# A mixture-of-experts stage whose down product goes from fp32 to three fp32r products, with the splits that this needs

## The reference

```python
for each expert e, on the rows routed to it:
    gu   = xs @ w_gu[e] + b_gu[e]                  # 1024 -> 2048
    gate = min(gu[:, :1024], 7);  up = clip(gu[:, 1024:], -7, 7)
    act  = gate * sigmoid(1.702 * gate) * (up + 1)
    out  = act @ w_down[e] + b_down[e]             # 1024 -> 1024
    y[token] += prob * out
```

## Time and profile before

| | us |
|---|---|
| median of 3 runs | 2609.05 |
| lowest and highest | 2608.40, 2609.14 |
| the profiled execution | 2608.08 |
| its span in the profile | 2606.5 |
| PE busy | 2402.0 (92%) |
| DVE busy | 1387.5 (53%) |
| ACT busy | 1117.0 (43%) |
| POOL busy | 587.7 (23%) |
| mean DMA rate | 232 GB/s, 604.43 MB |

### The profile page before, as it was taken

The page is one execution under the profiler, slowest core; times in us unless marked ns, Lnnn a source line. Parts: engine busy times, 40 slices in busy tenths (PEclk is TensorE's granted clock), DMA queues, the critical chain, the costliest instruction groups (busy, mean ns, idle before and its releaser), DMA issues. The chain is left out here.

```text
span 2606.5 us, 36290 instructions
## 1 busy us (share of the span) xinstructions
PE 2402.0 (92%) x11130; PEld 1541.8 (59%) x11131; DVE 1387.5 (53%) x1994; ACT 1117.0 (43%) x1443; POOL 587.7 (23%) x843
## 2 busy tenths in 40 slices
PE   8599999999976599999999999999999999999975
PEld 1177677777843356556556576666565665666641
DVE  0134445444334555555567566656575565666646
ACT  0023333333221445445455455555454554555532
POOL 0132333333221212112112122121221212121110
PEclk9799999999577799999999999999999999999985
DMA  8840000000021878777788789988787797989845
GB/s 307 334 161 33 33 32 32 32 28 3 29 68 38 318 293 296 262 275 282 261 333 331 296 322 348 359 306 309 281 335 284 249 370 263 353 330 366 341 162 220
DMA packets 142976, 604.43 MB, mean 232 GB/s; under 512 B 20128, under 2 KB 25261, under 8 KB 104469
## 3 DMA queue, kind: packets, MB, share of 16 engines
q1 hardware_dynamic: 120311, 551.51, 54.2%
q0 software_dynamic: 21968, 50.99, 8.1%
q10 hardware_dynamic: 662, 1.50, 0.2%
HBM read 561.82 MB, written 42.30 MB: 232 GB/s over the span
## 5 line engine op out<-in xcount | busy, mean ns | idle before, releaser
L1709 DVE TENSOR_TENSOR lo<-raw,hi 128x1024 fp32r<-128x1024 f32 x600 | 716.7, 1222 | 227.7 <-ACT hi L1645 201.5
L1645 ACT ACTIVATE hi<-raw 128x1024 fp32r<-128x1024 f32 x600 | 612.8, 1054 | 200.9 <-PE pg L1595 197.5
L1529 PE MATMUL py<-raw,aT 128*128 128x512 f32 x1184 | 537.9, 599 | 6.3 <-ACT aT L1657 6.3
L1592 PE MATMUL pg<-hi,xs 128*128 128x512 f32 x1184 | 475.4, 401 | 0.0
L1593 PE MATMUL pg<-lo,xs 128*128 128x512 f32 x1184 | 463.5, 391 | 0.0
L1595 PE MATMUL pg<-hi,xs 128*128 128x512 f32 x1184 | 368.1, 392 | 0.0
L1529 PEld LDWEIGHTS py<-raw,aT 128*128 128x128 f32 x1184 | 214.1, 190 | 250.6 <-issue 238.3
L1592 PEld LDWEIGHTS pg<-hi,xs 128*128 128x128 f32 x1184 | 222.5, 188 | 91.7 <-issue 46.7
L1595 PEld LDWEIGHTS pg<-hi,xs 128*128 128x128 f32 x1184 | 222.6, 188 | 50.0
L1593 PEld LDWEIGHTS pg<-lo,xs 128*128 128x128 f32 x1184 | 222.7, 188 | 45.0
L392 PE MATMUL X<-hT,w_in 128*128 128x128 f32 (+1 forms) x1728 | 225.4, 290 | 0.8 <-issue 0.8
(11 more groups left out here) (293 smaller groups left out, 2590.0 us busy)
## 6 DMA issues: line engine op xcount, KB each, us to landing
raw<-in_w_gu SPq DMA_DIRECT2D x300, 1024.0 KB, 7.3
raw<-in_w_down SPq DMA_DIRECT2D x148, 1024.0 KB, 6.9
wada<-in_w_ada SPq DMA_DIRECT2D x12, 2048.0 KB, 7.7
w_in<-in_w_in SPq DMA_DIRECT2D x5, 2048.0 KB, 14.2
moe_rows<-zero SPq DMA_DIRECT2D x9, 512.0 KB
x<-in_x_prompt SPq DMA_DIRECT2D x8, 512.0 KB
w_out<-in_w_out SPq DMA_DIRECT2D x1, 4096.0 KB, 24.8
xr<-in_x_prompt SPq DMA_DIRECT2D x8, 512.0 KB, 3.8
```

Source lines behind the costliest of these rows:

```text
L1529: return pe.matmul(py[n][:, :], aT[:, kt, :], raw[KT + kt // 2][:, kt % 2, n * 512:(n + 1) * 512], start=(kt == 0), stop=(kt == KT - 1))
L1592: pe.matmul(pg[u][b][:, :], xs[:, kt, 0, :], wh[:, u, :], start=False, stop=False)
L1645: act.activation(hi[q % RING][:, :, :], grain(q), ACT.Copy).then_inc(s["hi"], 1)
L1709: dve.tensor_tensor(lo[q % RING][:, :, :], grain(q), hi[q % RING][:, :, :].bitcast(F32), ALU.subtract).then_inc(s["lo"], 1)
```

## The change

All of it is in `experts`:

- An item has 24 grains now (`GRAINS = 3 * KT`): 16 of gate/up (`GU`), and eight of down, grain 16 + kt being row kt of raw8 to raw11. They go through the same rings, and `wait_used` asks for PE's use of a grain; for the last, grain 23, that is `y_mm1`, the end of the item's last product.
- `down` becomes `down_hi` (two products a half) and `down_lo` (one): 48 fp32r products an item in place of 16 fp32 ones.
- `aT` has a hi and a lo part; DVE makes the lo part with a new `act_lo`, once for each half.
- ACT splits grains 8 to 18 before the first swiglu (8 to 15 before), 19 and 20 after it, 21 to 23 later, and then grains 0 to 7 of the next item. DVE follows in the same order, and makes `sel` of the next item (`select`) ahead of the next item's grains, not behind them.
- In a T item PE does `tail_down` in two groups of 16 products, at kt 0 and 4, in place of four groups of 8.
- ACT copies both halves of the output. `y` is now `act1` itself, and the tail result goes to `pair`, a buffer that gate and up share; a wait for the scatter of the item before is added ahead of the tail's swiglu.
- Each item of ACT begins with a sigmoid of one value, `spark`.

```diff
-    GRAINS, RING = 2 * KT, 8
+    GU, GRAINS, RING = 2 * KT, 3 * KT, 8
...
+        sig, pair = sb("sigm", [P, 512]), sb("pair", [P, FF])
+        gate, up = pair[:, 0:512], pair[:, 512:1024]
-        aT = sb("aT", [P, FT, P])
-        y = sb("y", [P, D])
+        aT = sb("aT", [P, FT, 2, P], F32R)
+        y = act1
...
+        def chunk(q):
+            return ORDER[q][0] if q < GU else KT + (q - GU) // 2
...
+        def wait_used(eng, i, q):
+            if q < GRAINS - 1:
+                eng.wait_ge(s["used"], i * (GRAINS - 1) + q + 1)
+            else:
+                eng.wait_ge(s["y_mm1"], i + 1)
...
-            def down(i, kt, n):
-                return pe.matmul(py[n][:, :], aT[:, kt, :], raw[KT + kt // 2][:, kt % 2, n * 512:(n + 1) * 512],
-                                 start=(kt == 0), stop=(kt == KT - 1))
+            def down_hi(kt, n):
+                q = GU + kt
+                pe.matmul(py[n][:, :], aT[:, kt, 0, :], hi[q % RING][:, n, :], start=(kt == 0), stop=False)
+                pe.matmul(py[n][:, :], aT[:, kt, 0, :], lo[q % RING][:, n, :], start=False, stop=False)
+            def down_lo(kt, n):
+                return pe.matmul(py[n][:, :], aT[:, kt, 1, :], hi[(GU + kt) % RING][:, n, :], start=False, stop=(kt == KT - 1))
...
+                    pe.wait_ge(s["lo"], i * GRAINS + GU + kt + 1)
                     for n in range(2):
-                        last = down(i, kt, n)
-                    if kt % 2:
-                        last.then_inc(s["dn_done"], 1)
+                        down_hi(kt, n)
+                    if kt % 4 == 0:
+                        pe.wait_ge(s["alo"], i * 2 + kt // 4 + 1)
+                    for n in range(2):
+                        last = down_lo(kt, n)
+                    last.then_inc(s["used"], 1)
+                pe.wait_ge(s["lo"], i * GRAINS + GRAINS)
                 for n in range(2):
                     for kt in (KT - 2, KT - 1):
-                        last = down(i, kt, n)
+                        down_hi(kt, n)
+                        last = down_lo(kt, n)
+                        if n and kt == KT - 2:
+                            last.then_inc(s["used"], 1)
                     last.then_inc(s[f"y_mm{n}"], 1)
...
             def split_hi(i, q):
                 if q >= RING:
-                    act.wait_ge(s["gu_done"], i * GRAINS + q - RING + 1)
+                    wait_used(act, i, q - RING)
...
             def item(i, tail):
+                act.activation(spark[:, 1:2], spark[:, 0:1], ACT.Sigmoid)
...
-                for q in range(4, RING):
+                split_hi(i, GU + 7)
+                for q in range(RING):
                     split_hi(i, GRAINS + q)
                 if tail:
                     act.wait_ge(s["yt_mm"], i + 1)
                     for n in range(4):
-                        last = act.activation(act1[0:TAIL, n * W:(n + 1) * W], pg[1][0][n * TAIL:(n + 1) * TAIL, 0:W], ACT.Copy)
+                        last = act.activation(pair[0:TAIL, n * W:(n + 1) * W], pg[1][0][n * TAIL:(n + 1) * TAIL, 0:W], ACT.Copy)
                     last.then_inc(s["y_t"], 1)
                 act.wait_ge(s["y_mm0"], i + 1)
                 act.wait_ge(s["y_out"], i * 32 + 32)
                 act.activation(y[:, 0:512], py[0][:, :], ACT.Copy).then_inc(s["y0"], 1)
+                act.wait_ge(s["y_mm1"], i + 1)
+                act.activation(y[:, 512:1024], py[1][:, :], ACT.Copy).then_inc(s["y1"], 1)
...
+            def act_lo(i, b):
+                dve.wait_ge(s["aT"], i * 2 + b + 1)
+                dve.tensor_tensor(aT[:, b * 4:b * 4 + 4, 1, :], pt[0][:, :].rearrange("p (k t) -> p k t", k=4),
+                                  aT[:, b * 4:b * 4 + 4, 0, :].bitcast(F32), ALU.subtract).then_inc(s["alo"], 1)
```

More of the change, by code:

```diff
@@ L1613, in item @@
                         pe.wait_ge(s["aT"], i * 2 + 2)
-                    if tail and kt % 2 == 0:
+                    if tail and kt % 4 == 0:
                         if kt == 0:
                             pe.wait_ge(s["aT_t"], i + 1)
-                        tail_down(kt)
-                        tail_down(kt + 1)
-                    for n in range(2):
-                        last = down(i, kt, n)
-                    if kt % 2:
-                        last.then_inc(s["dn_done"], 1)
[L1623 to L1626, removed]
+                        for c in range(2):
+                            pe.wait_ge(s[f"raw{KT + kt // 2 + c}"], i * 16 + 16)
+                        for k in range(4):
+                            last = tail_down(kt + k)
+                        if kt:
+                            last.then_inc(s["yt_mm"], 1)
+                    pe.wait_ge(s["lo"], i * GRAINS + GU + kt + 1)
+                    for n in range(2):
+                        down_hi(kt, n)
[5 more added lines that the diff above has]
+                pe.wait_ge(s["lo"], i * GRAINS + GRAINS)
                 for n in range(2):
                     for kt in (KT - 2, KT - 1):
-                        last = down(i, kt, n)
+                        down_hi(kt, n)
+                        last = down_lo(kt, n)
+                        if n and kt == KT - 2:
+                            last.then_inc(s["used"], 1)
                     last.then_inc(s[f"y_mm{n}"], 1)
@@ L1640, in split_hi @@
             def split_hi(i, q):
-                kt, b = ORDER[q % GRAINS]
-                act.wait_ge(s[f"raw{kt}"], (i + q // GRAINS) * 16 + 16)
+                act.wait_ge(s[f"raw{chunk(q % GRAINS)}"], (i + q // GRAINS) * 16 + 16)
                 if q >= RING:
-                    act.wait_ge(s["gu_done"], i * GRAINS + q - RING + 1)
-                act.activation(hi[q % RING][:, :, :], grain(q), ACT.Copy).then_inc(s["hi"], 1)
+                    wait_used(act, i, q - RING)
+                act.activation(hi[q % RING][:, :, :], grain(q % GRAINS), ACT.Copy).then_inc(s["hi"], 1)
             def rows_hi(item, half):
@@ L1662, in item @@
                     act.activation(xs_t[:, :, :], pt[0][:, 0:KT * TAIL].rearrange("p (k t) -> p k t", k=KT), ACT.Copy).then_inc(s["xt"], 1)
-                for q in range(RING, GRAINS):
+                for q in range(RING, GU + 3):
                     split_hi(i, q)
@@ L1671, in item @@
                 squash(i, 0)
-                for q in range(3):
-                    split_hi(i, GRAINS + q)
+                for q in range(GU + 3, GU + 5):
+                    split_hi(i, q)
                 act_cols(i, 0)
@@ L1708, in split_lo @@
                 dve.wait_ge(s["hi"], i * GRAINS + q + 1)
[L1709 removed]
+                dve.tensor_tensor(lo[q % RING][:, :, :], grain(q % GRAINS), hi[q % RING][:, :, :].bitcast(F32), ALU.subtract).then_inc(s["lo"], 1)
             def rows_lo(item, half):
```

49 lines of the change are left out of this document (24 added, 25 removed).

## The result

The changed kernel takes **2631.8 us** (median of four runs, 2628.9 to 2632.2) where the kernel before took 2608.7 (2608.4 to 2609.1) on the same chip: ratio 1.0084, 95% interval 1.0069 to 1.0099, so it is slower by 0.8%. The forecast was 2589, the range ended at 2616. The profiled execution took 2631.49 us, its span 2629.9.

A forecast was written before the change was run, and what follows sets the result against it. TensorE (PE) was taken to set the pace in every item. Terms -103.6 + 22.5 + 38.2 + 20.4 + 2.4 = -20.1 us took the profiled 2608.08 to 2588.0; with the runs' median 1.0 higher, 2589 us, range 2561 to 2616.

The forecast's parts named there:

- Part 1: Down products on PE as 48 fp32r in place of 16 fp32: gain 2.80 us an item, 103.6 us in all.
- part 3: New PE wait for DVE's actm in N items: 0.9 us each, loss 22.5 us, N item 37.8 us.
- Part 2: Eight more splits an item on DVE and ACT: costed at nothing, DVE busy 36.4 us, ACT about 29.5.
- Part 4: PE waits at the end of T items for ACT's late tail copies: 3.55 or 2.45 us each, loss 38.2 us.
- Part 5: Clock drop after each of 12 gaps, at half of 3.4 us each: loss 20.4 us, bounds 0 and 41.
- the clock falls for twice as long: Rival: clock drops last twice as long, or also follow the 0.9 us waits: 2609 us, no change; chance 0.13.
- Part 6: The rest: output copies by ACT lose 2.4 us once; sigmoid nothing; selection free where it stands, a loss if moved.
- Part 7: Transfers: an N item's 13.8 MB need 36.3 us, under 37.8, so they cost nothing, by 1.5 us.
- slower, by transfers: Rival: weights arrive no faster than 348 GB/s, N items stay at 39.7 us: 2636 us; chance 0.07.

The follow-up runs named there:

- run 8: The changed kernel with ACT's tail copies ahead of the last four splits and the spark tile allocated last: 2535.8 us, ratio 0.9715.
- run 1: The changed kernel with ACT's four tail copies ahead of the last four of eight splits, not behind all eight: 2552.9 us, ratio 0.9786.
- run 5: The changed kernel with the 8-byte spark tile allocated behind all other tiles: 2612.0 us, ratio 1.0008.
- run 11: The changed kernel with DVE's selection put back behind the lo splits of the next item's first eight grains: 2855.6 us, ratio 1.0936.
- run 9: The kernel of run 8 with PE's transposes of the second actm half behind three down rows, not two: 2520.4 us, ratio 0.9661.
- run 2: The changed kernel with 24 useless transposes on PE at the end of each T item, tail copies still late: 2588.7 us, ratio 0.9919.
- run 12: The kernel of run 9 with the two branch bodies written in the other order, T body first: 2518.9 us, ratio 0.9658.
- run 10: The kernel of run 8 without the sigmoid on spark that begins each item's ACT work: 2535.1 us, ratio 0.9714.
- run 6: The kernel before with an unused 8-byte tile allocated ahead of idx: 2622.3 us, ratio 1.0052.
- run 7: The kernel before with an unused 16-byte tile ahead of idx, taking up the same 32 bytes as 8 would, on another chip: 2624.7 us, ratio 1.0048.

## Why the prediction was wrong, step by step

- **Part 1** (down products, -103.6) held in what it counted: run 8's N item is 37.79 us against the 37.8 of part 3, and its T item 50.12 against 50.43 (53.23 - 2.80). It was wrong in what it carried over. "Six take 1.37 us" was read from a kernel in which xs and aT lie elsewhere, and the new tile shifts them. The first step that failed is to take a pace as a property of the instruction: it was 1.40 in gate/up and down alike, **+17.1 us** (runs 1 and 8; 19.8 between the changed kernel and run 5, whose times are spread).
- **Part 2** held: DVE is busy for 35.80 us in an N item (forecast 36.4), ACT for 29.52 (29.5), and no idle time of PE is put down to lo. Run 11 shows how near the edge it is.
- **Part 3** held in kind and nearly in size: 0.7 us an item (run 9), not 0.9. In the sum this was covered by errors of the same size elsewhere in the item.
- **Part 4** held: 35.8 us against 38.2 (runs 1 and 2).
- **Part 5 is the step that failed most.** The drops came after all 12 gaps, as written. "At half of 3.4 us each" was the fault: 12 x 1.7 = 20.4 forecast, **43.2 measured** (run 2), which is 22.8 more. In the item shown 42.64 - 38.30 = 4.34 us are lost. Its upper bound, 41, which the measured 43.2 passes, was taken from one stretch of 6.8 us in a stage with shorter gaps. A gap of 3.4 us at the end of the item lay outside what those rows covered, and I put the likeliest value at the lowest of the cases seen. The rival "the clock falls for twice as long" (2609) was the nearest, with a chance of 0.13; its price of 20.4 us more was nearly right, but it was not joined with anything else.
- **The first item** was not foreseen: 4.75 us of gap and a clock at half for 10.3 us behind it. By run 12 it goes with the order of the bodies in the program; what makes PE stop there is open.
- **Part 6** held. The idle stretch of PE after the stage's last product grew from 22.89 to 26.24 us (3.35, forecast 2.4); the sigmoid is worth nothing (run 10), the selection's place 224 us (run 11).
- **Part 7** held: transfers set nothing. N items now run at 360 GB/s over 38.30 us, and run 9's at 368 over 37.09 with a share of 0.98; part of that is the scatter's and gather's traffic. The Trainium skill, "DMA: Bandwidth & Descriptors", section Specifications, gives about 358 GB/s as what HBM grants a core, half of what it gives for two. By that figure the N item would have been held at 38.6 us (an estimate, 13.8 MB over it). Run 9's 37.09 us, with one core of the chip in use, disagree with it. The share of 0.98 says that here there is little left.

Together: 2589 + 22.8 (clock) + 17.1 (placement) - 2.4 (part 4) + 1.0 (end) + 4.75 and some 5 of clock (first item, half of 10.2) = 2637; measured were 2631.8. Of the remaining 5 us some 4 are what T items came out shorter than forecast (0.31 x 12); the rest is open. All rivals changed one term at a time, and the range was their envelope; the result needed two misses of the same sign. The result's nearness to the 2636 us of the rival "slower, by transfers" is chance: no wait for transfers stands behind it.

## What to carry to other kernels

Ask of each wait put on TensorE what it costs behind its end as well as in it: gaps of 2.3 to 3.4 us cost 36 us here and the clock behind them 43, and a copy moved four places in ACT's order gave back both. Work added to an engine with slack pushes back everything queued behind it, so look for the short instruction that another engine waits for (tail copies: 79 us; selection: 224 us) before counting busy time. And when untouched code changes its pace, look at where tiles lie before and after: here, allocating the new small tile last put the others back where they had been, and the pace with them.

## What the runs showed of the hardware, unexpected

- **The pace of fp32r products depends on where tiles lie.** A small tile allocated ahead of xs and aT, which moves them by 32 bytes, takes six products from 1.37 to 1.40 us, and without it they are back at 1.37; the kernel before gets 0.5% slower by it (runs 5 to 7).
- **After short gaps the clock stays at the 1.2 GHz level for 3.4, 6.8 or 10.2 us while PE is busy.** How often it fell at the ends of T items: after 23 of 24 gaps of 2.3 to 3.4 us (the changed kernel and run 5), 6 of 8 of 2.0, 1 of 8 of 1.35, none of 1.0 or less. After gaps of up to 5.9 us it stayed there for up to 13.7 us (run 11).
- **PE's first entry into the second of two branch bodies stopped it for 4 to 6 us,** and the stop moved with the order of the bodies in the program (run 12). The kernel before has the same two bodies and did not show it.
